# Hybrid encoder on one core: the last expert pair's result returned by column halves

## The reference

```python
x = x + jnp.einsum('bsd,de->bse', merged, w_out[l])
x = x + hier_moe(rms_norm(x, ffn_norm_g[l]), ...)      # 32 experts, 2 for each token
...
z = jax.nn.silu(a) * u * cc[..., None]                 # a, u: gate and up products, width 256
y = jnp.einsum('cef,efd->cd', z, w_d)                  # down product, back to width 1024
```

## Time and profile before

| | us |
|---|---|
| median of 3 runs | 1304.12 |
| lowest, highest | 1303.5, 1305.22 |
| the profiled execution: its time | 1303.61 |
| its span | 1301.8 |
| PE busy | 1196.3 (92%) |
| DVE, ACT, POOL busy | 567.2, 408.6, 239.8 |
| mean granted clock of PE | 0.976 |

### The profile page before, as it was taken

How to read it: one execution, slowest core, us unless ns; L and a number is a source line. 1 busy time by engine, 2 the same in 40 slices (tenths; PEclk the granted TensorE clock), 3 DMA queues, 4 the chain that set the end, 5 groups by cost and what they waited for, 6 DMA issues and landing times.

```text
span 1301.8 us, 17478 instructions
## 1 busy us (share of the span) xinstructions
PE 1196.3 (92%) x6408; PEld 794.4 (61%) x6408; DVE 567.2 (44%) x1392; ACT 408.6 (31%) x822; POOL 239.8 (18%) x177
## 2 busy tenths in 40 slices
PE   7999998999999999889599999989999999988971
PEld 5777787888886343223177777778888853433320
DVE  4667865323345232112456677553234452222115
ACT  5444456333242110001244444562333411100002
POOL 0405320222200111111012254102221001111100
PEclk9999999999999999889899999999999999999996
DMA  5423321653666999999833333126437689999995
GB/s 201 118 81 98 98 82 35 210 192 97 240 229 245 404 424 422 423 422 411 315 98 88 89 113 98 43 93 217 160 99 279 217 301 422 424 422 427 417 412 221
DMA packets 69152, 305.51 MB, mean 235 GB/s; under 512 B 11798, under 2 KB 12054, under 8 KB 58832
## 3 DMA queue, kind: packets, MB, share of 16 engines
q1 hardware_dynamic: 58624, 282.45, 57.7%
q0 software_dynamic: 10304, 21.23, 4.5%
q10 hardware_dynamic: 144, 0.77, 0.2%
HBM read 288.63 MB, written 23.07 MB: 239 GB/s over the span
## 4 chain that ended last, share of the span: by engine, by line
PE 69%; DMA 12%; SPq 8%; ACT 4%; DVE 4%; issue 2%; DVEq 1%; POOLq 0%; ACTq 0%
PE bank L535 14%; PE bank L537 14%; PE bank L536 14%; PE bank L845 10%; DMA gu<-in_gu_w 9%; PE bank L861 5%; SPq L396 4%; SPq L401 3%; PE bank L644 2%; PE bank L673 2%; PE bank L608 1%; DMA raw<-in_stream 1%; PE bank L815 1%; PE bank L840 1%; PE bank L777 1%
## 5 line engine op out<-in xcount | busy, mean ns | idle before, releaser
L845 PE MATMUL bank<-gu,xgt 128*64 128x512 f32 x1024 | 239.7, 618 | 37.6 <-DMA gu<-in_gu_w 36.4
L535 PE MATMUL bank<-h_hi,w_hi 128*128 128x512 f32 x640 | 253.6, 396 | 4.4 <-DVE h_lo L1293 3.4
L537 PE MATMUL bank<-h_hi,w_lo 128*128 128x512 f32 x640 | 249.5, 390 | 0.0
L536 PE MATMUL bank<-h_lo,w_hi 128*128 128x512 f32 x640 | 249.2, 389 | 0.0
L1248 DVE TENSOR_TENSOR w_lo<-raw,w_hi 128x1024 fp32r<-128x1024 f32 x100 | 131.0, 1311 | 165.2 <-ACT w_hi L973 165.2
L845 PEld LDWEIGHTS bank<-gu,xgt 128*64 128x64 f32 x1024 | 75.0, 142 | 196.5 <-issue 149.6
L535 PEld LDWEIGHTS bank<-h_hi,w_hi 128*128 128x128 f32 x640 | 120.2, 188 | 30.3 <-DVE w_lo L1248 3.6
L537 PEld LDWEIGHTS bank<-h_hi,w_lo 128*128 128x128 f32 x640 | 120.1, 188 | 25.4
L536 PEld LDWEIGHTS bank<-h_lo,w_hi 128*128 128x128 f32 x640 | 120.3, 188 | 23.6
L973 ACT ACTIVATE w_hi<-raw 128x1024 fp32r<-128x1024 f32 x100 | 105.3, 1053 | 58.4 <-PE bank L537 54.9
L861 PE MATMUL bank<-dn,zt 128*64 128x512 f32 x512 | 116.9, 599 | 6.0 <-ACT zt L1209 2.8
(11 more groups left out here) (189 smaller groups left out, 1613.3 us busy)
## 6 DMA issues: line engine op xcount, KB each, us to landing
gu<-in_gu_w SPq DMA_DIRECT2D x18, 4096.0 KB, 31.1
raw<-in_stream SPq DMA_DIRECT2D x112, 512.0 KB, 3.6
dn<-in_dn_w SPq DMA_DIRECT2D x18, 2048.0 KB, 31.8
gu<-in_gu_w SPq DMA_DIRECT2D x32, 1024.0 KB, 13.9
dn<-in_dn_w SPq DMA_DIRECT2D x20, 1024.0 KB, 19.0
gu<-in_gu_w SPq DMA_DIRECT2D x32, 512.0 KB, 5.3
swp<-pj SPq DMA_DIRECT2D x136, 64.0 KB, 2.5
dn<-in_dn_w SPq DMA_DIRECT2D x16, 512.0 KB, 4.8
```

The source lines that it names most:

```text
L535: mm(dst, ah, bh, start=start, stop=False)
L536: mm(dst, ah, bl, start=False, stop=False)
L537: return mm(dst, al, bh, start=False, stop=stop)
L845: last = mm(bank[b][e * CAP:(e + 1) * CAP, :], xgt[:, x_s, k, e * CAP:(e + 1) * CAP], gu[w_s][:, e, k, :], start=k == 0, stop=k == KD - 1)
```

## The change

The last pair (n = 15) comes back in two column halves. PE waits for both parts of its down weights and then does all products of the left half, then all of the right half, and counts `dn_ok` up after each; so `dn_ok` rises by 17 a layer (`DOWNS`), not by 16. ACT copies the left half after the first, DVE the right half after the second. POOL scatters each half by itself, rows of 2 KB, with a view of `y_rows` of twice as many rows of half the width and doubled places, which DVE writes over the free entry 0 of `slot` with two more operations. The left one counts on a semaphore of its own (`left_ok`). SP loads the left halves of the second rows when that one has landed, in four DMAs of 256 KB, and the right halves, in four more, when the right one has; DVE adds four left halves and then four right ones, and only the right ones count up `x_ok`. `x_ld`, used for the load of x at the start, serves the right halves again, and the next layer's third weight tile waits for it. ACT gets one more wait before its second weight tile of the next layer.

```diff
@@ sync
-                def load_rows(k):
+                def load_rows(k, half, done):
                     for t in range(TT):
-                        sp.dma_start(yld[:, k, t, :], y_rows[k * T + t * P:k * T + (t + 1) * P, :]).then_inc(yl_ld[k][t], 16)
+                        sp.dma_start(yld[:, k, t, half], y_rows[k * T + t * P:k * T + (t + 1) * P, half]).then_inc(done[t], 16)
...
-                load_rows(0)
+                load_rows(0, slice(0, D), yl_ld[0])
...
-                for s in range(2):
-                    need(sp, ysc[s], (l + 1) * (PAIRS // 2) * 16)
-                load_rows(1)
+                need(sp, ysc[0], (l + 1) * (PAIRS // 2) * 16)
+                sp.wait_ge(left_ok, (l + 1) * 16)
+                load_rows(1, slice(0, T), yl_ld[1])
+                need(sp, ysc[1], (l + 1) * (PAIRS // 2) * 16)
+                load_rows(1, slice(T, D), x_ld)
@@ tensor
-                    if n in PARTS:
+                    if n == PAIRS - 1:
+                        for f in range(2):
+                            pe.wait_ge(dn_part[n][f], (l + 1) * 16)
+                        for half in range(2):
+                            for f in range(2):
+                                last = down_step(n % RING, half, f)
+                            last.then_inc(dn_ok, 1)
+                    elif n in PARTS:
@@ scalar
                     split_hi(l + 1, 0)
+                    act.wait_ge(dn_ok, (l + 1) * DOWNS)
                     split_hi(l + 1, 1)
@@ vector
+                        if n == PAIRS - 1:
+
+                            ts(slot[half, 0, :], bank[7][half, 2 * e:2 * e + 2], float(2 * T), 2.0, ALU.add, ALU.mult)
                         last = ts(slot[half, n, :], bank[7][half, 2 * e:2 * e + 2], float(2 * T), None, ALU.add)
...
-                for t in range(TT):
-                    dve.wait_ge(yl_ld[1][t], (l + 1) * 16)
-                    stt(x[:, t, :], yld[:, 1, t, :], w_second[:, t:t + 1], x[:, t, :], ALU.mult, ALU.add).then_inc(x_ok, 1)
+                for half, done, times in ((slice(0, T), yl_ld[1], l + 1), (slice(T, D), x_ld, l + 2)):
+                    for t in range(TT):
+                        dve.wait_ge(done[t], times * 16)
+                        last = stt(x[:, t, half], yld[:, 1, t, half], w_second[:, t:t + 1], x[:, t, half], ALU.mult, ALU.add)
+                        if done is x_ld:
+                            last.then_inc(x_ok, 1)
@@ gpsimd
-                for n in range(PAIRS - 4, PAIRS):
+                for n in range(PAIRS - 4, PAIRS - 1):
...
+                def scatter_half(half, done):
+                    pool.indirect_dma_start(out=y_halves, out_offset=bass.IndirectOffsetOnAxis(ap=slot[:, 0, 0:1].bitcast(U32), axis=0),
+                                            in_=yb[1][:, half * T:(half + 1) * T], in_offset=None, element_offset=half * T,
+                                            bounds_check=4 * T - 1, oob_is_err=False).then_inc(done, 16)
+
+                pool.wait_ge(ya_ok, n0 + PAIRS)
+                scatter_half(0, left_ok)
+                pool.wait_ge(yd_ok, n0 + PAIRS)
+                scatter_half(1, ysc[1])
```

More of the change, by code:

```diff
@@ L37 @@
 MORE_AT = {s: sum(1 for n in WHOLE if n % RING == s) for s in range(RING)}
+DOWNS = PAIRS + 1
 PARAMS = KD * NLOG + NLOG + 2 * KD + 8
@@ L129, in hybrid_encoder @@
     y_rows = nc.dram_tensor("y_rows", (2 * T, D), FP32, kind="Internal").ap()
+    y_halves = y_rows.rearrange("r (h n) -> (r h) n", h=2)
     h2_rows = nc.dram_tensor("h2_rows", (T, D), FP32, kind="Internal").ap()
@@ L272, in hybrid_encoder @@
         cst_ld, par_ld, gr_ld = sems("cst_ld", "par_ld", "gr_ld")
-        x_ld = sems(*(f"x_ld{t}" for t in range(TT)))
         raw_ld = sems("raw_ld0", "raw_ld1")
@@ L314, in hybrid_encoder @@
             "gu_ok", "sil_ok", "z_ok", "zt_ok", "zte_ok", "dn_ok", "ya_ok", "yd_ok")
+        x_ld = sems(*(f"x_ld{t}" for t in range(TT)))
         yl_ld = [sems(*(f"yl_ld{k}_{t}" for t in range(TT))) for k in range(2)]
+        left_ok = sem("left_ok")
         warm_ok, fin_ok, out_st = sems("warm_ok", "fin_ok", "out_st")
@@ L434, in _ @@
                     if i == 2 and l:
-                        sp.wait_ge(yl_ld[1][TT - 1], l * 16)
+                        sp.wait_ge(x_ld[TT - 1], (l + 1) * 16)
                     if i >= 2 or l == 0:
@@ L463, in _ @@
                 load_gu_part(l, 3, 3)
-                sp.wait_ge(dn_ok, l * PAIRS + 1)
+                sp.wait_ge(dn_ok, l * DOWNS + 1)
                 load_dn_part(l, 3, 0)
@@ L473, in _ @@
                         load_gu(l, p)
-                    sp.wait_ge(dn_ok, l * PAIRS + p - RING + 1)
+                    sp.wait_ge(dn_ok, l * DOWNS + p - RING + 1)
                     if p in PARTS:
@@ L481, in more_experts @@
                 def more_experts(r, p, q):
-                    sp.wait_ge(dn_ok, (l + 1) * PAIRS)
+                    sp.wait_ge(dn_ok, (l + 1) * DOWNS)
                     need(sp, ov_sc, q * 16)
@@ L492, in _ @@
                 need(sp, ov_sc, total * 16)
-                def load_rows(k):
+                def load_rows(k, half, done):
                     for t in range(TT):
-                        sp.dma_start(yld[:, k, t, :], y_rows[k * T + t * P:k * T + (t + 1) * P, :]).then_inc(yl_ld[k][t], 16)
-                sp.wait_ge(dn_ok, (l + 1) * PAIRS - 1)
+                        sp.dma_start(yld[:, k, t, half], y_rows[k * T + t * P:k * T + (t + 1) * P, half]).then_inc(done[t], 16)
+                sp.wait_ge(dn_ok, l * DOWNS + PAIRS - 1)
                 for s in range(2):
                     need(sp, ysc[s], ((l + 1) * (PAIRS // 2) - 1) * 16)
-                load_rows(0)
+                load_rows(0, slice(0, D), yl_ld[0])
                 if l + 1 < L:
@@ L1199, in y_half @@
                 def y_half(n):
-                    act.wait_ge(dn_ok, n0 + n + 1)
+                    act.wait_ge(dn_ok, l * DOWNS + n + 1)
                     need(act, ysc[n % 2], (l * (PAIRS // 2) + n // 2) * 16)
@@ L1575, in y_half @@
                 def y_half(n):
-                    dve.wait_ge(dn_ok, n0 + n + 1)
+                    dve.wait_ge(dn_ok, l * DOWNS + n + (2 if n == PAIRS - 1 else 1))
                     need(dve, ysc[n % 2], (l * (PAIRS // 2) + n // 2) * 16)
```

## The result

The changed kernel takes 1310.98 us (median of 13 runs, 1307.53 to 1313.44), the kernel before 1304.72 (13 runs on the same chips): ratio 1.0043, 95% interval 1.0032 to 1.0054. That is 5.6 us slower (4.2 to 7.0). Slower was forecast, by 2.7 us, with 1309.0 as the upper end.

A forecast was written before the change was run, and what follows sets the result against it. The chain of waits was mostly PE; at the layer ends, ACT's late squares were to decide. Layer 0 +2.3 and layer 1 +0.4 made +2.7 on 1303.6, so 1306.3, named as 1306.5 us; range 1303.5 to 1309.0.

The forecast's parts named there:

- The sign and the mechanism: Both layer ends: slower by 2.7 us, with gapless half additions, late first x_ok and four squares back to back.
- The work stays 3.68, as the same 16 passes: PE's last down products: they start later but still take 3.68 us.
- The hold: PE before the last down products: waiting for both down parts delays them 1.3 us in layer 0, 1.25 in layer 1.
- the clock as a rival: PE's constant matmuls before the last transposes: clock still at 1.2 GHz, 1.1 to 2.9 us more, 1307.4 to 1309.2; chance 0.12.
- So they are hidden, with 1 to 2 us to spare; cost nothing: Halved loads of second rows: they land before DVE wants them, 1 to 2 us to spare, no cost.
- The rival that the second down part is no hindrance: PE's last down products: second part there in time; layer 0 costs 1.0, layer 1 gains 0.85, 1303.8; chance 0.15.
- The faster rival: DVE's wait for second rows: transfers decide, gain 1.15 to 2.5 us a layer, say 1300; chance 0.06.
- The third term: ACT's squares at both layer ends: they queue after the right halves; layer 0 +2.3 us, layer 1 +0.4.

The follow-up runs named there:

- e4: Changed kernel with one constant matmul of 128x512 between PE's waits for the first and second down part; ratio 1.0029, +3.8 us against the kernel before.
- e2: Changed kernel with the last pair's down products part by part again, the rest halved as in the change; ratio 1.0025, +3.3 us against the kernel before.
- e8: Changed kernel with products part by part and whole-row additions, scatter and loads still halved; ratio 1.0046, +6.0 us against the kernel before.
- e6: Kernel before with only the additions of second rows by column halves, four left then four right; ratio 1.0050, +6.5 us.

## Why the prediction was wrong

*The sign and the mechanism* held. DVE's second additions without a gap in layer 0, the first `x_ok` late, four squares in a row and the last transposes behind them are all in the trace of the changed kernel, though in layer 1 DVE waited a little for loads. From the ready point the first square was forecast at 17.6 and came at 19.2. Of the 1.6, 1.3 is the clock. The squares themselves were a little quicker than forecast, about 1.04 apart instead of 1.24: the 1.24 that I had read as ACT's pace in the earlier trace rows was DVE's, as the last two squares there began when their tiles had just been added.

*"The work stays 3.68, as the same 16 passes"* is the step that failed. The hold was sized right (products start 1.4 after the ready point), but the 1.3 to 1.7 us by which the products stretch at 1.2 GHz were missing, at one end in the first trace and at both in the second. Over the two traces that is 2.4 us for a kernel. I had the clock as a rival, but at the wrong place, at the constants behind the additions. There it was low as well, the constants took 6.38, and the transposes of four tiles stood in one piece behind them. The clock was up again by then, so the rival as I had put it did not happen, but the queue cost some 0.6 us: PE ended 2.6 after DVE had scaled tile 3, where it was 2.0 before.

*"So they are hidden, with 1 to 2 us to spare; cost nothing"* failed in size. I took the loads by halves at the pace of whole ones, and they take 1.5 to 2 us longer. I also had the left loads issued 8.9 after the ready point, and they were at 9.3, behind the weight tiles. In layer 0 of the changed kernel the held and slowed products covered that. In e4, where the clock stays up, DVE waits for them, and its ends are +2.8 and +0.9 over the mean of the two traces of before, 3.8 together where the forecast had 2.7. So the two misses overlap and must not be added. For the changed kernel the ends are +4.4 together in the first trace and +5.4 in the second; the interval of the measured +5.6, 4.2 to 7.0, holds both.

*The rival that the second down part is no hindrance* (1303.8) is what e2 makes true by construction, and e2 is +3.3 (1.2 to 5.3), not +0.2. Its price left out the loads, too. *The faster rival* has its premise refuted: e8 shows left loads only 0.3 us earlier than whole ones at either end, where the rival had 0.6 with the hold and 1.95 without, and the halved loads then take longer than that saves.

*The third term*, the late squares, was right in kind: e6, with no hold and whole transfers, shows that additions in the order left, then right can cost 6.5 us by themselves. Its size within the change was not isolated.

## What to carry to other kernels

Splitting the last transfer of a chain pays only if the consumer can use a part. Here the sum of squares needs the row, so work by column halves turned a pipeline over tiles into a queue; the kernel before, which goes by tiles, was faster than every version with halved scatters, loads or additions. Splitting along the tiles, not across what is reduced, suggests itself, but a finer split of that kind was not tried. A reordering of matmuls that waits for a later DMA costs the wait and can cost the clock; cheap constants in the wait kept it. And before counting on an earlier small DMA, look at what is queued ahead of it.

## What the runs showed of the hardware that I had not expected

- A wait of PE of 1.7 to 1.9 us ahead of the last down products brought its clock to half in 5 of 6 cases, and the products from 3.65 to 5.0 to 5.4 us. A wait as long ahead of the last gate and up products of layer 1 did so in 1 of 16.
- A scatter of 128 rows of 2 KB landed no sooner than the whole one while 1 MB of other loads was queued: 5.0 against 4.2 us from its start; without those loads the whole one took 3.05. In layer 1, with less queued ahead, the loads followed the left scatter of the changed kernel by 3.2 and the whole one by 2.9, so half the bytes did not land sooner there either.
- One of the 16 DMA engines ended the weight tiles about 2 us after the others, and a scatter issued behind them got its last count only after that.
- DMAs of 64 partitions with 4 KB rows took 11.5 us for 2 MB where those of 128 took 8.5.
- The squares of 128x1024 that waited for nothing follow each other at 1.04 us on ACT; those that began when their tile had just been added had 1.24, the pace of the additions.
